# One layer with routed experts on one core: VectorE's index arithmetic one block ahead, the last stage's residual inputs loaded during the last expert, its shaping on three engines

## The reference, cut to what matters

```python
# D_MODEL 1024, SEQ 1024 tokens, 32 experts in 4 groups, top 1 group, top 2 experts in it, D_EXPERT 512
p_group = softmax(t @ w_rg + b_rg); p_g, grp = top_k(p_group, 1)
logits_in = (t @ w_re + b_re).reshape(n_tok, 4, 8)[grp]
p_e, local = top_k(softmax(logits_in), 2)
gate = p_g * p_e / sum(p_e); expert = grp * 8 + local
# rows sorted by expert into blocks, each block owned by one expert
yb = (silu(xb @ w_gate[e]) * (xb @ w_up[e])) @ w_down[e]
y = sum of gate * yb over the two picks of a token
# and at the end of the layer
x = layer_norm(alpha * x + g2 * y, ln2_g, ln2_b)      # alpha = 2 ** 0.25
```

## Time and profile before

| what | value |
|---|---|
| median of 3 runs | 1745.64 us (1744.97 to 1746.34) |
| the profiled execution's own time | 1749.57 us |
| span of the profiled execution | 1747.8 us |
| mean granted TensorE clock | 0.943 |
| experts, first matmul of `hidden` to the barrier | 1199 to 1687 us |
| combine | 1687 to 1747.8 us |
| SP's longest wait in the experts' loads, on ScalarE's copies of the down matrices | 164.4 us in 12 waits |

### The profile page before, as it was taken

One profiled execution on the slowest core, in us unless ns is written; L12 is line 12 of the kernel. 1 busy time (PEld: TensorE's weight loads), 2 busy tenths in 40 slices (PEclk: granted clock), 3 DMA queues, 4 the chain that ended last, 5 costly groups with the idle time before them and its releaser, 6 DMA issues. The chain is left out here.

```text
span 1747.8 us, 47291 instructions
## 1 busy us (share of the span) xinstructions
PE 1518.8 (87%) x19436; PEld 1104.0 (63%) x19436; DVE 933.1 (53%) x1867; ACT 687.4 (39%) x1580; POOL 179.4 (10%) x261
## 2 busy tenths in 40 slices
PE   5799998999968899979998889946999999998858
PEld 3588785779857888856666667733555555554433
DVE  5798743331125566559999657772142353344317
ACT  5544431112244545437667634422141443333310
POOL 0000100000054454300000000001000000000020
PEclk9899998999968999989999999957999999999889
DMA  9322415550243344230110053229567979999947
GB/s 357 121 69 78 129 46 195 186 172 9 69 129 95 117 133 118 76 125 19 43 43 19 7 177 146 97 100 369 211 251 283 338 287 398 395 391 397 356 143 294
DMA packets 154396, 305.33 MB, mean 175 GB/s; under 512 B 10718, under 2 KB 57390, under 8 KB 150834
## 3 DMA queue, kind: packets, MB, share of 16 engines
q1 hardware_dynamic: 132306, 244.94, 38.7%
q0 software_dynamic: 10336, 46.67, 7.5%
q10 hardware_dynamic: 11520, 10.49, 1.9%
HBM read 256.40 MB, written 45.66 MB: 173 GB/s over the span
## 5 line engine op out<-in xcount | busy, mean ns | idle before, releaser
L2711 PE MATMUL psum<-now_hidden,i_xm 128*32 128x256 f32 x4992 | 296.0, 388 | 33.3 <-DVE now_hidden L2805 27.4
L2711 PEld LDWEIGHTS psum<-now_hidden,i_xm 128*32 128x32 f32 x4992 | 158.6, 112 | 163.3 <-DVE now_hidden L2805 43.1
L2723 PE MATMUL psum<-now_down,i_hT 128*32 128x256 f32 x2464 | 147.4, 379 | 2.2 <-ACT now_down L2768 2.2
L2815 DVE TENSOR_TENSOR i_h<-i_silu,psum 128x128 f32<-128x128 f32 x78 | 22.3, 286 | 207.8 <-ACT i_silu L2761 207.8
L2805 DVE COPY now_hidden<-raw_hidden 128x1024 f32 x168 | 103.2, 689 | 52.6 <-PE psum L2711 25.6
L2753 ACT ACTIVATE i_xm<-psum,modT 128x128 f32<-128x128 f32 x163 | 63.4, 457 | 167.3 <-issue 135.6
L2723 PEld LDWEIGHTS psum<-now_down,i_hT 128*32 128x32 f32 x2464 | 81.0, 110 | 55.0 <-ACT now_down L2768 4.4
L1911 PE MATMUL psum<-dkT,f_qT 64*128 64x512 f32 (+1 forms) x384 | 91.1, 581 | 23.6 <-ACT f_E L1962 21.1
L123 PE MATMUL psum<-hT_head,wm_head 128*128 128x512 f32 (+1 forms) x256 | 96.8, 378 | 11.3 <-DVE hT_rest L414 6.9
L1962 ACT ACTIVATE f_E<-psum,f_mx 128x1280 f32<-128x1280 f32 (+2 forms) x96 | 92.1, 968 | 15.7 <-DVE f_mx L2021 15.5
L123 PE MATMUL psum<-hT_rest,wm_head 128*128 128x512 f32 (+1 forms) x256 | 95.1, 372 | 0.0
(11 more groups left out here) (373 smaller groups left out, 2971.7 us busy)
## 6 DMA issues: line engine op xcount, KB each, us to landing
raw_hidden<-in_w_gate SPq DMA_DIRECT2D x22, 2048.0 KB, 20.0
raw_hidden<-in_w_up SPq DMA_DIRECT2D x22, 2048.0 KB, 23.8
raw_down<-in_w_down SPq DMA_DIRECT2D x22, 2048.0 KB, 20.5
wa_late<-in_w_ada POOLq DMA_DIRECT2D x16, 1024.0 KB, 5.5
yb<-i_y ACTq DMA_DIRECT2D x80, 128.0 KB, 7.1
wa<-in_w_ada SPq DMA_DIRECT2D x8, 1024.0 KB, 13.6
wt<-in_w_in SPq DMA_DIRECT2D x4, 2048.0 KB, 7.8
wm<-in_w_in SPq DMA_DIRECT2D x12, 512.0 KB, 3.7
```

The source lines that it names most:

```text
L2711: last = nc.tensor.matmul(by_blocks(hidden_bank(s)[j * SUB:(j + 1) * SUB, :]), xm[u][:, k, s * SUB:(s + 1) * SUB], columns_of(now["hidden" ...
L2723: last = nc.tensor.matmul(down_bank(s)[j * SUB:(j + 1) * SUB, :], hT[s % 2][:, k * SUB:(k + 1) * SUB], now["down"][:, k, j * WIDE:(j + 1) ...
```

## The change

It has two parts. **In experts**, VectorE reads `ranks` and works out the semaphore counts and the slot one block earlier: `look(b + 3)` stands behind the copies of body b and ahead of its `mix`, and the next body's copies start from values that are already in registers. From the quad q = 17 on the first body of each quad works them out anew before its copies. Gate and up of a slot share one semaphore, so VectorE waits for three counts and not six. SP's waits for the slots are as before; only two of its register reads now come ahead of the second expert's loads.

**In combine**, the eight residual tiles and the norm rows lie where the raw slots were (`COLD`), and SP loads them during the experts phase, after the copies of the last expert's gate and up, ahead of the stores of zeros. TensorE does the residual product of a tile first, for the first four tiles before it waits for any gather, and for tile t of the last four after tile t - 4 was centred. For tiles 2 to 6 the last multiply is done by ScalarE and the last add by GpSimd; tiles 0, 1 and 7 stay on VectorE.

```diff
+    def hidden():
+        if copied and place is not SLOTS - 1:
+            sp.wait_ge(copied["hidden"], (place - (SLOTS - 1)) * KD)
+        load("gate", raw["hidden"][:, h, 0, :, :], loaded["hidden"][h])
+        load("up", raw["hidden"][:, h, 1, :, :], loaded["hidden"][h])
+    def down():
         if copied:
-            if n == "down":
-                sp.wait_ge(copied["down"], (place - 1) * CHUNKS["down"])
-            elif u > 2 or place is not u:
-                sp.wait_ge(copied["hidden"], (place - 2) * CHUNKS["hidden"])
+            sp.wait_ge(copied["down"], (place - 1) * KE)
+        load("down", raw["down"][:, u % 2, :, :], loaded["down"][u % 2])
...
+    x1 = m.keep["x1"] = [nc.alloc_sbuf_tensor_at(f"j_x1{t}", [P, D], F32, offset=COLD + 4 * D * t) for t in range(TL)]
+    rep_ln = m.keep["late_ln"] = nc.alloc_sbuf_tensor_at("j_rep_ln", [P, 2, D], F32, offset=COLD + 4 * D * TL)
...
+            sp.wait_ge(copied["hidden"], experts_ * KD)
+            for t in range(TL):
+                sp.dma_start(x1[t][:, :], d["x1"][t]).then_inc(early, 16)
+            sp.dma_start(rep_ln[:, :, :], d["rep_ln"].rearrange("p (w n) -> p w n", w=4)[:, 2:4, :]).then_inc(early, 16)
             sp.wait_ge(nothing_ready, 1)
...
-            def copy_hidden(place, b):
-                for n in ("gate", "up"):
-                    wait_loaded(dve, n, place)
-                loaded = hidden_slot(place)
+            def copy_hidden(at, counts, b):
+                for first in range(SLOTS):
+                    dve.wait_ge(loads["hidden"][slot_of(first)], counts[first])
+                loaded = raw["hidden"][:, bass.ds(at, 1), :, :, :].rearrange("p a w k n -> p (a w) k n")
                 for k in range(KD):
                     dve.wait_ge(used["hidden"], b * KD + k + 1)
                     nc.vector.tensor_copy(now["hidden"][:, :, k, :], loaded[:, :, k, :]).then_inc(copied["hidden"], 1)
+            def look(b):
+                place = place_of(dve, b)
+                counts = [nc.vector.snap((third(place + SLOTS - first) + (1 if first else 0)) * 32) for first in range(SLOTS)]
+                return place, nc.vector.snap(hidden_slot(place)), counts
...
             def body(q, i, u, s):
                 b = q * SUBS + s
-                after, later = (place_of(dve, b + n) for n in (1, 2))
+                if q > LOW and s == 0:
+                    ahead[:] = [place_of(dve, b + 1), look(b + 2)]
+                after, (later, at, counts) = ahead
                 with dve.If(after < later):
-                    copy_hidden(after + 1, b + 1)
+                    copy_hidden(at, counts, b + 1)
+                ahead[:] = [later, look(b + 3)]
                 mix(b + 1, (s + 1) % SUBS)
                 keep_y(b, i, u, s)
...
+    HELD = 4
+    BY_POOL = (2, 3, 4, 5, 6)
...
+            for t in BY_POOL:
+                pool.wait_ge(scaled, BY_POOL.index(t) + 1)
+                nc.gpsimd.tensor_tensor(acc[t][:, :], acc[t][:, :], rep_ln[:, 1, :], ALU.add).then_inc(pool_ready, 1)
...
+            pe.wait_ge(early, 16 * (TL + 1))
+            def residual(t):
+                for here in halves:
+                    nc.tensor.matmul(sums(t)[:, here], by_alpha[:, :], x1[t][:, here], start=True, stop=False)
+            for t in range(HELD):
+                residual(t)
             for t in range(TL):
+                if t >= HELD:
+                    pe.wait_ge(centred, t - HELD + 1)
+                    residual(t)
                 pe.wait_ge(gathered[t], 32)
-                pe.wait_ge(loaded[t], 16)
-                if t >= 4:
-                    pe.wait_ge(taken, t - 3)
...
+                for here in halves:
+                    nc.tensor.matmul(sums(t)[:, here], by_gate[:, 0, t, :], y1[t][:, here], start=False, stop=False)
+                    nc.tensor.matmul(sums(t)[:, here], by_gate[:, 1, t, :], y2[t][:, here], start=False, stop=True).then_inc(summed, 1)
...
+            def scale(t):
+                act.wait_ge(inverted, t + 1)
+                act.wait_ge(centred, t + 1)
+                nc.scalar.activation(acc[t][:, :], acc[t][:, :], ACT.Identity, scale=sd[t][:, :]).then_inc(scaled, 1)
             for t in range(TL):
                 deviation(t)
+                if t in BY_POOL:
+                    scale(t)
```

More of the change, by code:

```diff
@@ L2363, in routing @@
     raw = m.keep["raw"]
-    m.keep["raw_loaded"] = {n: [m.sem(f"w_{n}_loaded{u}", lasting=True) for u in range(2 if n == "down" else SLOTS)] for n in ("gate", "up", "down")}
+    m.keep["raw_loaded"] = {n: [m.sem(f"w_{n}_loaded{u}", lasting=True) for u in range(k)] for n, k in (("hidden", SLOTS), ("down", 2))}
     rep_g = m.keep["rep_g"] = m.sb("rep_g", [P, D // SUBS])
@@ L2406, in _ @@
             sp.wait_ge(planned, 1)
-            load_expert(m, sp, 0, 0)
+            for part in expert_loader(m, sp, 0, 0):
+                part()
             sp.wait_ge(gate_loaded, 16 * SUBS)
@@ L2631, in third, with wait_down_loaded @@
         return (value * 43) >> 7
-    def wait_loaded(eng, n, place):
-        if n == "down":
-            eng.wait_ge(loads[n][0], ((place >> 1) + 1) * 16)
-            eng.wait_ge(loads[n][1], (((place + 1) >> 1) + 1) * 16)
-            return
-        for first in range(SLOTS):
-            eng.wait_ge(loads[n][slot_of(first)], (third(place + SLOTS - first) + (1 if first else 0)) * 16)
+    def wait_down_loaded(eng, place):
+        eng.wait_ge(loads["down"][0], ((place >> 1) + 1) * 16)
+        eng.wait_ge(loads["down"][1], (((place + 1) >> 1) + 1) * 16)
     def down_slot(place, k):
@@ L2666, in _, with follow @@
         def _(sp):
-            load_expert(m, sp, 1, 1)
             experts_ = sp.value_load(plan[0:1, PLAN_EXPERTS:PLAN_EXPERTS + 1], min_val=2, max_val=NE)
             nq = sp.value_load(plan[0:1, PLAN_QUADS:PLAN_QUADS + 1], min_val=LOW, max_val=QUADS)
+            def follow(place, u):
+                for part in expert_loader(m, sp, place, u, copied if u > 1 else None):
+                    part()
+            AHEAD = 2 * SLOTS
+            follow(1, 1)
             with sp.If(2 < experts_):
-                load_expert(m, sp, 2, 2, copied)
-            AHEAD = 2 * SLOTS
+                follow(2, 2)
             with sp.Fori(0, (NE - 3 + AHEAD - 1) // AHEAD) as i:
@@ L2822, in body @@
                 b = q * SUBS + s
-                after, later = (place_of(dve, b + n) for n in (1, 2))
+                if q > LOW and s == 0:
+                    ahead[:] = [place_of(dve, b + 1), look(b + 2)]
+                after, (later, at, counts) = ahead
                 with dve.If(after < later):
-                    copy_hidden(after + 1, b + 1)
+                    copy_hidden(at, counts, b + 1)
+                ahead[:] = [later, look(b + 3)]
                 mix(b + 1, (s + 1) % SUBS)
                 keep_y(b, i, u, s)
-            for n in ("gate", "up"):
-                for first in range(1, SLOTS):
-                    dve.sem_inc(loads[n][slot_of(first)], 16)
-            for n in ("gate", "up"):
-                dve.wait_ge(loads[n][slot_of(0)], 16)
+            for first in range(1, SLOTS):
+                dve.sem_inc(loads["hidden"][slot_of(first)], 32)
+            dve.wait_ge(loads["hidden"][slot_of(0)], 32)
             for k in range(KD):
                 nc.vector.tensor_copy(now["hidden"][:, :, k, :], raw["hidden"][:, slot_of(0), :, k, :]).then_inc(copied["hidden"], 1)
-            here, after = place_of(dve, 0), place_of(dve, 1)
+            here, (after, at, counts) = place_of(dve, 0), look(1)
             with dve.If(here < after):
-                copy_hidden(here + 1, 0)
+                copy_hidden(at, counts, 0)
+            ahead = [after, look(2)]
             mix(0, 0)
```

87 lines of the change are left out of this document (39 added, 48 removed).

## The result

The changed kernel takes 1733.8 us (median of 8 runs, 1729.67 to 1740.08) against 1745.31 us for the kernel before in the same comparison (8 runs): ratio 0.9938, 95% interval 0.9927 to 0.995, which is 10.8 us less by the ratio and 11.5 by the medians. Two further comparisons gave 0.9943 (0.9928 to 0.9958) and 0.9956 (0.9939 to 0.9974). The prediction said 1727.9, so the direction and the outer range (1723.5 to 1737.5) held. The likeliest case's own range, 1725.5 to 1730.5, did not: of 17.7 us, some 11 came.

A forecast was written before the change was run, and what follows sets the result against it. Engines pace experts up to about 1427, the weights' transfers from there. Experts 9.6 plus combine 8.1 give 17.7 us, median 1745.64 to 1727.9; likeliest case (55%) 1725.5 to 1730.5, outer range 1723.5 to 1737.5.

The forecast's parts named there:

- Removed gap, hidden `look`: Experts, VectorE: visible gap before copies falls to 0.1 us; `look`, some 1.5 us, costs nothing in bodies with copies.
- three waits on ready registers: Experts, new body: with a branch and one slot address, all that is left before the copies, put at 0.4 us.
- Rival 1: Experts: `look` is not hidden, 1.5 us go serially between copies and `mix`; 1733.3 us, chance 10%.
- The first run gives back 4.0, the second 3.9: Experts: gains in the first two runs of three one-block experts, 0.2 us a run left for ScalarE.
- the trigger: Experts, third run: the `keep_y` that ScalarE awaits before SP's down load comes 1.7 us earlier, restarting the DMA engines.
- From there 223 us of transfers stand as they are: Experts after the DMA restart: the saturated stretch keeps its length, so the end comes 9.6 us earlier.
- The barrier comes 7.6 us behind: End of experts: barrier 7.6 us behind ScalarE's last stores, which move from 1679.43 to 1669.8.
- The early loads cost nothing: End of experts: nine DMAs, 5.2 MB, and the zeros take 19 us at 392 GB/s; cover 12 us, cost nothing.
- combine 8.1 us: Combine: TensorE starts when the diagonals are ready and ends at 1732.7, not 1740.8; gain 8.1 us, bounds 6.4 to 8.5.
- Rival 5: Combine: all passes as slow as the first four; chance 3%.
- GpSimd's add: Combine: the last add of a tile on GpSimd takes 2.1 us, twice the 512 column row.
- rival 4: End of combine: GpSimd's add meets tile 7's centring on VectorE, end up to 2.1 us later; 1730 us, chance 8%.

The follow-up runs named there:

- fewer_bytes: The changed kernel without the up-matrix loads of three experts (places 6, 12 and 18), 6 MB less moved: 1725.94 us, ratio 0.9889 to the kernel before.
- look_in_place: The changed kernel with the register work put back directly ahead of the copies, all else new: 1742.89 us, ratio 0.9963 to the kernel before.
- look_alone: The changed kernel's new experts part without the early loads, with the old combine: 1741.28 us, ratio 0.9959 to the kernel before.

## Why the prediction was right or wrong

**Removed gap, hidden `look`: right.** Visible gap 0.1 us forecast; 0.38 and 0.18 measured before the second and third copies, and of the 0.38 some 0.3 are TensorE's chunk, as forecast. `look` lies inside the copies and takes 1.2 us (1.5 forecast). One premise was wrong at no cost: "three waits on ready registers". The counts are not ready, they are worked out at the waits, so that from the branch to the third copy (1416.3 to 1417.0) 0.7 us pass and not 0.4, most of it beside `keep_y`. Rival 1 (`look` not hidden) gave 1733.3, which is within 0.5 us of the result, and its mechanism is refuted. A time that fits a rival does not prove it; the row of `mix` without a bracket decides. That the total lies inside the outer range is owed to combine: the experts phase gave 4.5 of the 9.6 us forecast.

**"The first run gives back 4.0, the second 3.9": this term was too large.** They gave back 2.4 and 2.9 (means of the traces), and the trigger, with the rest of the way to the restart, 1.3 and not 1.7: the restart comes 6.6 us earlier and not 9.6. I had named ScalarE as next late and left 0.2 us for it, because I summed ScalarE's work in a body (5.0 us) and took its inputs as ready. Two things came late. The first is the down matrix of the long expert behind each run. Its load can't be issued before the down copies of the last but one expert are done, and ScalarE's copies, which waited for it, began 8.0, 9.4 and 9.0 us after its issue. Before, the run's own slowness hid that, with 0.6, 3.0 and 0.2 us to spare. A run that is shorter by 4 us brings ScalarE to that landing 2 to 3 us too early; chunking the load brought back 3.8 us at the last copies. The second is the quad's end: 1.8 us of store issues and two reads of `ranks` stand before ScalarE's input part, so that its copies start late: in the two chunked traces TensorE's `down` waits 0.3 to 0.7 us for them in the first and third run; putting the stores behind brought the first run from 23.3 to 22.6.

**"From there 223 us of transfers stand as they are": right.** 223.3 and 223.1 before, 223.5, 223.1 and 223.1 in the three traces of the changed kernel. fewer_bytes shows the bytes as the bound, with little room: of 10.7 us of transfers left out 5.3 came through (6.0 counted from the restart), and SP waited more for copies.

**"The barrier comes 7.6 us behind" the last stores, and 9.6 earlier in all: this failed too, and here the cause stays open.** The last matmul to the first gather took 9.0 and 9.4 us before, and 11.4 to 13.3 in the changed kernel: 2.9 us lost. Some 1.8 of them are there without early loads and with the zeros first, too. What the traces show is that ScalarE's sequencer is slow for some us there: the last four stores take 5.0 to 5.3 us in the changed kernel (3.7 to 5.5 in all kernels with the new experts code but look_in_place) and not 2, and in the three traces of the changed kernel two reads of `ranks` ahead of them take 0.5 to 1.53 us each, which otherwise take 0.3. look_in_place has normal last stores (1.81 us) and the slow patch one body earlier. It goes with every variant that has any part of the change. One thing stands beside it in the traces and was not tested: in the fourteen traces together 103 of ScalarE's 164 stores and reads of `ranks` in experts that took over 0.7 us overlap a transfer of the instruction queue q8, and 481 of the 3043 that took under 0.5 us. A longer one also has more chance to, so this is a lead and no cause.

**The early loads cost nothing: right to within about 1 us.** They lie in a window at a DMA share of 0.92; the last expert's matmuls end 27.0 to 27.4 us behind its copies, and 27.5 in look_alone, which has none; the first gather may come up to 1 us later for them, as said above.

**combine 8.1 us: right.** Measured 8.1 between the means, though the time at the lower clock level, before the passes speed up, varies between executions: 3.3 and 6.1 us in the two of before, 3.2, 5.0 and 3.6 in the three of the changed kernel. The clock granted at that level is 0.50 and behind it 1.00: so in 1696.1 to 1699.3 and 1699.4 to 1741 of the first trace of before, and in 1683.2 to 1686.3 and 1686.4 to 1726 of the first of the changed kernel. My bound of 8.5 belongs to three slow passes; two would give 9.0. TensorE's first pass comes 2.7 us behind the barrier's end, sixteen residual passes take 8.69 us (forecast 8.6), the last ends 45.7 us behind the barrier, and the tail is 6.9 us (7.0). In this trace the clock was granted as in the first trace of before: the first four passes take 3.4 us in both, the rest come 0.43 us apart. The 1740.8 of the sum is the end of the chain's last row, 1725.13 + 15.70, and the chain's 0.436 is 15.70 / 36. Rival 5, all passes of combine as slow as the first four, did not come: the 96 passes were busy for 43.02 us at a granted clock of 0.94 between the first gather and the last pass.

**GpSimd's add, 2.1 us forecast, took 2.35.** The last one ended at 1727.03, and tile 7's centring began at 1727.22. So rival 4 had 0.2 us of room left and did not come. VectorE's centring takes 1.284 us in both kernels. The adds lay beside operations that read PSUM: the centrings at 1707.48 and 1711.77 ran beside an add and took 1.28 us as the others. What an add beside a VectorE instruction with two SBUF inputs costs is not shown: in none of the ten traces with the adds does such an instruction run beside one. An earlier phase has such a pair, with a multiplication for the add. In the trace of before VectorE's 128 x 128 subtraction of two SBUF inputs (L1583, 20 times), each time beside a multiplication on GpSimd (L1310), takes from 0.248 to 0.547 us for the same shape. No case without GpSimd beside it stands there to compare, so the cause of that spread is not shown.

The sum as it came, from the traces: 6.6 + 0.8 - 2.9 + 8.1 = 12.6 us, where I had 9.6 + 8.1 = 17.7. By the medians the three comparisons gave 11.5, 10.9 and 7.2.

## What to carry to other kernels

When a stall is removed from a loop, look up every transfer whose landing the stall used to hide, and by how much it was on time: here the next wait was a load with 0.2 to 3.0 us to spare, and no row of idle time pointed to it. Chunking both the reuse of a buffer and the load into it took this wait away; it brought the last copies forward by 3.8 us, of which the traces' sums keep 2.2. If a consumer is moved to the front of a stage, its inputs have to be there: with the nine loads issued at the start of the stage, beside the gathers, the same order took 19 us more.

## What the runs showed that I had not expected

Reads of a register from SBUF, 0.30 us each, took up to 1.53 us on ScalarE near the end of the phase (0.92 was the most in the trace of before), and single store issues 1.5 to 3 us where 0.45 is usual, at a time when the DMA engines were a third busy (share 0.35). The first run of one-block experts starts anywhere from 1265.4 to 1275.9 us in the fourteen traces, a spread as large as the effect of the whole change, and from 1267.6 to 1272.2 in the three of one and the same kernel; only distances within the trace could tell the variants apart.
